# Expert rows of the two middle blocks: 18 of 128 summed on VectorE in place of TensorE

## The reference, cut to what matters

```python
eid = e1 * PEER_NKEYS + e2                      # 8 heads x 16 = 128 experts a token
gate = softmax(sc)
act = gelu(einsum('td,thkd->thk', xb, u_tab[eid]))
return einsum('thk,thkd->td', gate * act, v_tab[eid])
```

## Time and profile before

| | us |
|---|---|
| runs, median (lowest to highest) | 1781.21 (1778.16 to 1781.8) |
| the profiled execution, its time | 1780.13 |
| its span | 1777.7 |
| TensorE matmul busy | 1538.4 (87%) |
| VectorE busy | 1062.2 (60%) |
| ScalarE busy | 604.7 (34%) |
| GpSimd busy | 576.6 (32%) |

### The profile page before, as it was taken

The page is one execution under the profiler, slowest core; times in us unless marked ns, Lnnn a source line. Parts: engine busy times, 40 slices in busy tenths (PEclk is TensorE's granted clock), DMA queues, the critical chain, the costliest instruction groups (busy, mean ns, idle before and its releaser), DMA issues.

```text
span 1777.7 us, 18617 instructions
## 1 busy us (share of the span) xinstructions
PE 1538.4 (87%) x6020; PEld 921.1 (52%) x6020; DVE 1062.2 (60%) x2499; ACT 604.7 (34%) x1759; POOL 576.6 (32%) x561
## 2 busy tenths in 40 slices
PE   8999988999877778998899978998999968777776
PEld 7779977764322225763456525663457523222222
DVE  1584634577888875334556447665556468874444
ACT  1434411233333333227532323346632323332222
POOL 2000000244444442233432442334432444443441
PEclk9999958999999999999999999999999999999999
DMA  6222003899999999999999999999999999999996
GB/s 250 96 74 93 1 1 111 342 411 427 426 427 427 426 427 422 427 426 427 427 424 425 421 427 425 427 426 427 427 382 426 397 426 427 427 427 427 427 427 275
DMA packets 92063, 638.32 MB, mean 359 GB/s; under 512 B 11072, under 2 KB 13120, under 8 KB 15424
## 3 DMA queue, kind: packets, MB, share of 16 engines
q0 software_dynamic: 73728, 536.90, 71.8%
q1 hardware_dynamic: 18240, 100.24, 14.4%
HBM read 636.05 MB, written 1.05 MB: 358 GB/s over the span
## 4 chain that ended last, share of the span: by engine, by line
PE 52%; DMA 34%; ACT 6%; DVE 6%; issue 3%; POOL 1%; ACTq 0%; SPq 0%; POOLq 0%; DVEq 0%
DMA arena<-l_peer_uv,arena 33%; PE psum L905 22%; PE psum L587 14%; PE psum L886 5%; DVE arena L1715 3%; PE psum L764 2%; PE psum L809 1%; PE psum L680 1%; PE psum L670 1%; PE psum L679 1%; ACT L1202 1%; POOL arena L554 1%; ACT arena L1207 1%; ACT early L1215 1%; ACT arena L1215 1%
## 5 line engine op out<-in xcount | busy, mean ns | idle before, releaser
L554 POOL DMA_INDIRECT arena<-l_peer_uv,arena x512 | 563.4, 1100 | 1089.3 <-PE psum L905 828.9
L1715 DVE CUSTOM_DVE_ANT_0 arena<-arena,xres 128x1024 f32<-128x1024 f32 x512 | 619.3, 1223 | 406.5 <-DMA arena<-l_peer_uv,arena 400.9
L905 PE MATMUL psum<-arena,early 128*128 128x512 f32 x1024 | 477.6, 611 | 99.8 <-ACT early L1215 96.4
L905 PE MATMUL psum<-arena 128*128 128x512 f32 x1024 | 474.5, 608 | 95.7 <-ACT arena L1215 92.2
L905 PEld LDWEIGHTS psum<-arena,early 128*128 128x128 f32 x1024 | 189.4, 193 | 359.5 <-issue 200.4
L905 PEld LDWEIGHTS psum<-arena 128*128 128x128 f32 x1024 | 189.1, 192 | 354.8 <-issue 210.4
L587 PE MATMUL psum<-xT,wring 128*128 128x128 f32 (+2 forms) x1856 | 295.9, 319 | 12.5 <-DMA wring<-l_w_in 8.2
L587 PEld LDWEIGHTS psum<-xT,wring 128*128 128x128 f32 (+1 forms) x1856 | 268.5, 191 | 51.6 <-issue 21.1
L1202 ACT ACTIVATE arena<-arena 128x2 f32<-128x2 f32 x256 | 52.0, 203 | 595.4 <-DVE arena L1715 595.1
L1030 ACT COPY arena<-psum 128x256 f32<-128x256 f32 (+2 forms) x138 | 62.5, 472 | 220.8 <-PE psum L587 117.3
L1207 ACT ACTIVATE arena<-arena 128x1 f32<-128x1 f32 x512 | 123.3, 287 | 23.8
(11 more groups left out here) (236 smaller groups left out, 1142.7 us busy)
## 6 DMA issues: line engine op xcount, KB each, us to landing
wring<-l_w_in SPq DMA_DIRECT2D x47, 1024.0 KB
wring<-l_peer_wq SPq DMA_DIRECT2D x24, 1024.0 KB
wring<-l_w_out SPq DMA_DIRECT2D x12, 1024.0 KB
arena<-l_peer_uv,arena POOLq DMA_INDIRECT x512
ln_par<-l_ln_g SPq DMA_DIRECT2D x6, 512.0 KB
ln_par<-l_ln_b SPq DMA_DIRECT2D x6, 512.0 KB
arena<-l_peer_keys SPq DMA_DIRECT2D x2, 1024.0 KB, 6.9
xT<-x_t SPq DMA_DIRECT2D x1, 1024.0 KB, 4.8
```

The costliest lines, as they stand in the source:

```text
L554: pool.indirect_dma_start(out=ring[:, g % RING, :], out_offset=None, in_=T[f"l{l}_peer_uv"], in_offset=bass.IndirectOffsetOnAxis(ap=eid[:, ...
L905: last = mm(self.ps[c], diag[k % DIAGS], ring[:, g % RING, D + c * 512:D + (c + 1) * 512], start=not self.begun, stop=True, skip_group_che ...
L1715: v.tensor_tensor_reduce(out=u, in0=u, in1=xres[:, self.b, :], scale=1.0, scalar=0.0, op0=ALU.mult, op1=ALU.add, accum_out=hid[:, self.b, ...
```

## The change

One function. In blocks 1 and 2, the slots 11, 15, 19, ..., 79 (18 in each) are now summed on VectorE.

```diff
 def on_vector(n, s):
 
-    return False
+    return n in (1, 2) and 8 <= s < 80 and s % 4 == 3
```

## The result

The changed kernel takes 1785.70 us, median of 12 runs (1779.53 to 1790.22), the kernel before 1780.88 in the 12 runs beside them (1776.54 to 1782.41). The ratio is 1.0026 with a 95% interval of 1.0014 to 1.0037: slower by 4.6 us (2.5 to 6.6). The forecast was no change (1780.5), so it was wrong in direction, though the time lies within the range of 1776.5 to 1788.

The account below looks back on a forecast made before the run. Bound by DMA at its ceiling to about 1300 us, TensorE's chain to 1415, then DMA again. Terms +1.3 and -2.0 (the +1.0 inside the latter) gave -0.7 us, so 1780.5 as median; range 1776.5 to 1788.

Parts of the forecast that it names:

- Step 4: Attention of block 2: TensorE's wait grows to 2.34 us, steps stay 10.3 us, VectorE's addition falls in a pause; 0.
- Strips: Slots 11 to 39 of both blocks: DMA stays the pace and VectorE has room for the additions; 0.
- `combine` of block 1: Two additions ahead of the layer norm delay TensorE's next rows and the gathers behind them; +1.3 us, between 0 and 1.4.
- Slot 39: Ahead of block 2's attention: VectorE's addition delays TensorE's logits and the first attention step; +1.0 us, between 0 and 1.37.
- rival (a): TensorE's clock falls after longer waits in both blocks' attention, three falls in block 2; slower, 1786.6 us; chance 0.24.
- The ring: Gather queue in block 2's attention: rows are released later, but 1.3 us remain and the queue stays fed; 0.
- Rival (b): Rows held longer by VectorE dry up the gather queue, and GpSimd contends with its additions; slower, 1784.5 us; chance 0.10.
- The tail: End of block 2: slots 75 and 79 leave TensorE's chain between output strips, less DMA time lost; -2.0 us.
- (c): Delays at block 1's `combine` and before block 2's attention hide, block 2's tail gives full price; faster, 1776.8 us; chance 0.16.

Follow-up runs that it names:

- kernel 5: The changed kernel with the attention's eight rows back on TensorE, 10 slots a block left on VectorE; median 1783.0 us, ratio 1.0014 to before.
- kernel 4: The changed kernel with the 18 slots on VectorE in block 2 only, block 1 as before; median 1785.3 us, ratio 1.0037 to before.
- kernel 8: The kernel before with only slots 45, 49, ... 73 of block 2 (attention, behind TensorE's wait) on VectorE; median 1781.0 us, ratio 0.9997.
- kernel 15: The kernel before with only slots 43, 47, ... 71 of block 2 (attention, ahead of TensorE's wait) on VectorE; median 1783.9 us, ratio 1.0017.
- 3: The changed kernel with ROW_LAG 1 in place of 2, so VectorE uses rows up a pair earlier; median 1787.9 us, ratio 1.0056 to before.
- kernel 13: The kernel before with slots 43, 47, ... 71 of block 1 on VectorE, zero-weight filler products on TensorE, ROW_LAG 1; median 1785.4 us, ratio 1.0022.
- 7: The changed kernel with slots 9, 13, ... 77 in place of 11, 15, ... 79, both blocks; median 1777.6 us, ratio 0.9993 to before.
- 9: The kernel before with slots 9, 13, ... 77 of block 2 alone on VectorE; median 1781.0 us, ratio 1.0004.
- 2: The changed kernel with each of VectorE's weighted row additions cut to 16 columns from 512; median 1785.4 us, ratio 1.0027 to before.
- 11: The kernel before with only slots 43, 47, ... 71 of block 1 on VectorE, plus the two additions ahead of block 2's norm; median 1786.4 us, ratio 1.0028.
- kernel 1: The changed kernel with filler, four zero-weight products on TensorE at each slot VectorE sums; median 1782.9 us, ratio 1.0026 to before.
- 12: The kernel before with slots 43, 47, ... 71 of block 1 on VectorE and zero-weight filler products on TensorE at each; median 1784.6 us, ratio 1.0023.
- 16: The kernel before with slots 43, 47, ... 71 of block 2 on VectorE and zero-weight filler products on TensorE at each; median 1782.6 us, ratio 1.0008.
- 14: Slots 43, 47, ... 71 of block 1 on VectorE with TensorE filler, and more filler at both blocks' attention exits; median 1790.0 us, ratio 1.0041 to before.

## Why the prediction was wrong, step by step

Two steps failed. Step 4 put the attention of block 2 at 0 because a wait of 2.34 us seemed too short for a fall of the clock; and the sum had no term at all for the attention of block 1, on the ground that landings hide what happens there.

**1. Strips: 0.** Held. At slot 48 of block 1 nothing has been lost or won, and kernel 5 loses nothing there. An addition took 747 ns, not 680:

```profile
L1734 DVE SCALAR_TENSOR_TENSOR masks<-arena,masks 128x512 f32<-128x512 f32 x68 | 48.0, 747 | 0.0
```

**2. `combine` of block 1: +1.3.** Right in the mean over profiles (1.3), wrong as a fixed price: each profile has either nothing or 1.5 to 2.8, so that the number fits is in part luck. The profile after shows 2.3, and why it can exceed the 1.37 us of the additions: the wait of 2.84 us of the earlier trace rows is there too, and the eight matmuls behind it took 6.13 us in place of 5.40.

```profile
1083.87 6.13 PE L905 MATMUL psum<-arena 128*128 128x512 f32 x8 [2.84 <-ACT arena L1215]
```

**3. Slot 39: +1.0.** Held, as far as two profiles tell. In kernel 4, whose block 2 starts as before, the landings grow 0.9 late between slots 48 and 56. In kernel 5, which has no row of the attention on VectorE and no fall in it, D is 1.1.

**4. The attention of block 2: 0.** The reading of the chain held: steps of 10.3 with a wait of 2.34, and kernel 8 shows it from the other side. What failed is the use of the sentence that 2.34 us of waiting is "below every wait that a fall followed". It was true of the profile before and of no other: kernel 15 falls twice after exactly 2.34 us, and in block 1 falls follow 2.08 (the earlier trace rows had shown one wait of 2.43 without a fall; one row, of which the view shows five of eight matmuls, is no bound). Two falls in the profile after cost 3.3 us in this block, where I had put 0; in kernel 15, by itself, the row ahead of the wait cost 3.0 us (0.9 to 5.0).

**Block 1's attention** is where the largest loss of the profile is, 5.9 us, and the sum had no term for it. This is the second step that failed. The waits there are 2.08 to 2.48 us and not the 3.1 of rival (a), and most bring a fall even so. In rival (a) I had written that landings hold its steps and hide most. They hide it only while the queue has a lead. The steps with a fall take 10.65 us and drop behind the gathers' 9.8 one after the other. At the end of the attention come strips and rows, where TensorE is busy throughout; at slot 84 the queue had a lead of 3.9 us before and has 1.5 in the change, and the hole at 910 opened. "Hidden by a landing" was true of each step and false of the eight together.

**5. The ring: 0.** Nothing was lost to held rows by themselves: kernels 3 and 13 give them back and are not faster, and 7 holds them longer and is. Rival (b) is out. Its other argument did not come true either: GpSimd's busy time did not rise beside the additions (576.6 us before, 573.8 after).

**6. The tail: -2.0.** Mis-sized in its parts. GpSimd's wait is still there, 8.50 us to a gather at 1312.47 (10.19, to 1305.09). Of the two rows one counts: the logits of the last attention step are 7.4 us later than before, the last burst of rows (1404.29 against the 1398.80 of the earlier trace rows) 5.5, so the chain got 1.9 back, not 3.4. Slot 79's share went into a wait for a strip:

```profile
1310.48 1.72 PE psum L905 x4
1312.19 3.47 PE psum L886 x16
1315.68 9.95 DMA wring<-l_w_out
1325.67 3.73 PE psum L886 x16
```

The last window of the earlier trace rows did not come up to 427 but to 393, though all work in it is some 6 us later than in the same window before. Kernel 5, with the same two rows and no falls in block 2's attention, ends the chain 0.24 us earlier than before.

**Rivals.** (a) came closest: 1786.6 forecast, 1785.7 measured, with the clock as its carrier, but with two falls in block 2, not three, and the larger part in block 1, not 1 us: that its number fits so well is luck. (c) is out.

**What stays open.** That the row ahead of the wait is what costs is shown by timed runs (change against 7, 4 against 9, 15 against 8); that VectorE's time and held rows are not, also (2; 3, 7 and 13). That falls go with the losses at A and D is shown in the profiles: in four kernels without filler (the change, 2, 3, 11) A is 2.9 to 5.9, in 1 and 12 it is 0, in 13 it is 3.2 behind a fall of another place, in 16 D is 0.3. Kernels 7 and 14 lie between, with A at 2.1 and two low stretches in the attention of block 1, and at 1.4 and one. The fit is not perfect: kernel 1 has one too, at 863.5, and loses nothing. But the means of the timed runs with filler are lower only by 1.1 (change to 1, +-1.3), 0.0 (11 to 12, +-1.4) and 1.2 us (15 to 16, +-0.8; standard errors of the differences). None of the three is clear of noise. For block 2 the size can be reconciled with the clock; for block 1, where 3 to 6 us should have come back, it can't. So that the clock's falls make the 4.6 us of the timed runs is argued from profiles and not shown. The filler kernels lose something else, in part in the two additions at C (1.3), and 14 is later still than 12 (by 2.4, +-1.6). B (1.2 in 1, 1.7 in 12) is not the filler's, since kernel 5 loses 1.7 there without it. I have no cause for the upper group. Of the profiles of filler kernels that of 12 (1790.0 us) is the latest; 4.0 us of its lateness stood before block 1 began, ahead of all that was changed. The losses are not additive either: by the ratios, 4 and 11 together would be 11.6 us, the change costs 4.6.

## What to carry to other kernels

Before moving work off an engine, find the wait in its loop: work taken from ahead of the wait only lengthens it, work taken from behind it shortens the step. A longer wait is not free on TensorE: here the clock fell behind many of the longer waits, and the eight matmuls behind took 5.40 us in place of 3.70. A single wait without a fall is no proof of safety. Lateness "hidden by the DMA" adds up over a stage; compare it with the queue's lead at the point where that stage ends.

## What the runs showed of the hardware that I had not expected

- Falls of the clock after short waits: eight matmuls of 3.70 us took 5.40 after 2.08 and after 2.34 us. In block 2 of the profile after, five waits of 2.34 and 2.35 us were followed by 3.70 and one of 2.35 by a fall, and in kernel 15 a wait of 2.48 us (to 1241.99) was followed by 3.70, so the wait alone does not decide. In kernel 13 the clock fell at 902.7 after waits of 0.4 to 1.1 us between short products.
- The clock and the time of single runs go together even in the kernel before: in its five sets of 23 or 35 runs the correlation of time with mean granted clock is -0.62 to -0.75, 0.8 to 1.0 us for each 0.001. Which of the two makes the other is not shown.
- Where the filler raised the mean clock from 0.957 to 0.967 (change to 1), the mean time came down by 1.1 us only (+-1.3): clock regained is not of itself time regained.
- A two-input operation of VectorE with 512 columns whose result overwrites an input took 747 ns, more than the 688 of another two-input operation of 512 columns and more than half of the 1284 of its own form with 1024.
